# Moving two heads' score products side by side in TensorE's order, in a two-block transformer kernel

## The reference

```python
mod_x = jnp.split((jax.nn.silu(c) @ ada_w[layer] + ada_b[layer])[:, None, :], 6, axis=-1)
...
s = jnp.einsum('bqhd,bnhd->bhqn', q, k).astype(jnp.float32) * (HEAD_DIM ** -0.5)
p = jax.nn.softmax(s, axis=-1)
...
return jnp.einsum('bhqn,bnhd->bqhd', p.astype(v.dtype), v)
```

## Time and profile before

| | |
|---|---|
| median of three runs | 3044.91 us (3044.56 to 3044.98) |
| profiled execution, its time | 3045.68 us |
| its span | 3043.9 us |
| TensorE matmul busy | 2769.8 us (91%) |
| GpSimd busy | 1871.4 us (61%) |
| ScalarE busy, VectorE busy | 1490.2 us (49%), 1044.2 us (34%) |
| mean granted clock | 0.952 |
| at0, first scores to last transposed output | 219.6 to about 400.9 us |
| at1, the same | 932.6 to about 1056.7 us |

### The profile page before, as it was taken

How to read it: one execution, slowest core, us unless ns; L and a number is a source line. 1 busy time by engine, 2 the same in 40 slices (tenths; PEclk the granted TensorE clock), 3 DMA queues, 4 the chain that set the end, 5 groups by cost and what they waited for, 6 DMA issues and landing times.

```text
span 3043.9 us, 54209 instructions
## 1 busy us (share of the span) xinstructions
PE 2769.8 (91%) x19868; PEld 2566.2 (84%) x19868; DVE 1044.2 (34%) x2456; ACT 1490.2 (49%) x2604; POOL 1871.4 (61%) x789
## 2 busy tenths in 40 slices
PE   4999999999988989998889987899888899889897
PEld 2887778999976789997889987899878899778897
DVE  3124534111144521224333364333342333442334
ACT  4326744434444544444455565455545455454555
POOL 5426646878854668872458855388634588524685
PEclk8999999999998999998999998999999999989998
DMA  6224434545533445541235533255423355313453
GB/s 237 90 70 146 139 111 139 180 162 183 184 112 111 166 137 182 186 153 63 98 126 183 181 118 109 92 170 182 138 77 111 106 184 179 125 56 111 135 182 125
DMA packets 115044, 421.48 MB, mean 138 GB/s; under 512 B 12768, under 2 KB 13792, under 8 KB 114400
## 3 DMA queue, kind: packets, MB, share of 16 engines
q1 hardware_dynamic: 114336, 413.39, 40.5%
q10 hardware_dynamic: 576, 6.23, 0.5%
HBM read 418.52 MB, written 1.05 MB: 138 GB/s over the span
## 4 chain that ended last, share of the span: by engine, by line
issue 43%; PE 28%; POOL 25%; DVE 3%; ACT 1%; POOLq 1%; ACTq 0%; DVEq 0%
POOL ring_low L1922 25%; PE bank L544 8%; PE bank L545 8%; PE bank L546 8%; PE bank L725 1%; PE bank L752 1%; PE bank L660 1%; PE bank L657 1%; POOLq L1925 0%; DVE rstd L1416 0%; PE bank L768 0%; ACT ring_high L1014 0%; PE bank L739 0%; ACT scr L1111 0%; POOLq L1921 0%
## 5 line engine op out<-in xcount | busy, mean ns | idle before, releaser
L1922 POOL TENSOR_TENSOR ring_low<-ring,ring_high 128x1024 fp32r<-128x1024 f32 x785 | 1871.2, 2405 | 1150.0 <-ACT ring_high L1014 790.0
L544 PE MATMUL bank<-high,ring_high 128*128 128x256 f32 (+1 forms) x4052 | 1210.1, 299 | 148.6 <-DVE low L1478 73.0
L545 PE MATMUL bank<-low,ring_high 128*128 128x256 f32 (+1 forms) x4052 | 1191.5, 294 | 0.0
L546 PE MATMUL bank<-high,ring_low 128*128 128x256 f32 (+1 forms) x4052 | 1190.5, 294 | 0.0
L544 PEld LDWEIGHTS bank<-high,ring_high 128*128 128x128 f32 x4052 | 800.5, 198 | 172.8 <-DVE low L1478 77.3
L545 PEld LDWEIGHTS bank<-low,ring_high 128*128 128x128 f32 x4052 | 800.6, 198 | 10.8 <-issue 1.2
L546 PEld LDWEIGHTS bank<-high,ring_low 128*128 128x128 f32 x4052 | 799.8, 197 | 8.7
L1212 ACT ACTIVATE ring_high<-ring 128x1024 fp32r<-128x1024 f32 x462 | 479.0, 1051 | 33.9 <-PE bank L544 33.9
L1014 ACT ACTIVATE ring_high<-ring 128x1024 fp32r<-128x1024 f32 x323 | 334.7, 1052 | 124.6 <-PE bank L544 93.5
L544 PE MATMUL bank<-hid_high,ring_high 128*128 128x256 f32 x1232 | 351.0, 285 | 9.7 <-DVE hid_low L1683 9.7
L545 PE MATMUL bank<-hid_low,ring_high 128*128 128x256 f32 x1232 | 350.3, 284 | 0.0
(11 more groups left out here) (177 smaller groups left out, 2970.1 us busy)
## 6 DMA issues: line engine op xcount, KB each, us to landing
ring<-in_units SPq DMA_DIRECT2D x785, 512.0 KB, 3.3
xt<-in_x ACTq DMA_DIRECT2D x1, 2048.0 KB, 13.9
nbias<-in_bias ACTq DMA_DIRECT2D x1, 1536.0 KB, 8.1
consts<-in_consts ACTq DMA_DIRECT2D x1, 1472.0 KB, 8.2
vt<-in_mem ACTq DMA_DIRECT2D x1, 1024.0 KB, 7.6
out_x<-xt SPq DMA_DIRECT2D x8, 128.0 KB, 1.7
cols<-in_cols SPq DMA_DIRECT2D x1, 711.0 KB, 8.0
```

What stands on the lines that cost most here:

```text
L544: first = pe.matmul(out, w[0], x[0], start=start, stop=False, **more)
L545: pe.matmul(out, w[0], x[1], start=False, stop=False, **more)
L546: return first, pe.matmul(out, w[1], x[0], start=False, stop=stop, **more)
L1922: pool.tensor_tensor(whole(ring_low, u), whole(ring, u), whole(ring_high, u).bitcast(fp32), ALU.subtract).then_inc(unit_ready, 1)
```

## The change

TensorE's order: `scores(s+1, 1)` moves up behind `scores(s+1, 0)`, ahead of the transposes of head 1, and the modulation products of slot 3s, which stood between the two heads' scores, move behind the transposes of head 1. ScalarE's order: the copy of head 1's transposed probabilities moves ahead of `exps(s+1, 0)`, and `exps(s+1, 1)` moves ahead of the work of slot 3s+1. VectorE's, GpSimd's and SyncE's orders stay as they are. Only at0 and at1 (`shallow`) change; for the other attentions the order comes out as before.

```diff
@@ TensorE, attention @@
                         transposes(s, 0)
                         if shallow:
                             scores(s + 1, 0)
-                            fill(3 * s)
+                            scores(s + 1, 1)
                         transposes(s, 1)
-                        if shallow:
-                            scores(s + 1, 1)
-                        else:
+                        if not shallow:
                             scores(s + 2, 0)
                             scores(s + 2, 1)
+                        fill(3 * s)
                         if s:
                             out_t(s - 1)
@@ ScalarE, attention @@
                         out_pt(s, 0)
+                        out_pt(s, 1)
                         if shallow:
                             exps(s + 1, 0)
-                            ada_rest(3 * s)
-                        out_pt(s, 1)
+                        ada_rest(3 * s)
                         if s:
                             out_high(s - 1)
...
-                        ada_rest(3 * s + 1)
                         if shallow:
                             exps(s + 1, 1)
                         else:
                             exps(s + 2, 0)
                             exps(s + 2, 1)
+                        ada_rest(3 * s + 1)
                         ada_rest(3 * s + 2)
```

## The result

The changed kernel takes 3083.43 us (median of four runs, 3079.72 to 3095.89) against 3044.73: 38.7 us slower. The ratio of all runs together is 1.0135, 95% interval 1.0105 to 1.0165 (the two medians alone give 1.0127). The prediction was 3059, with 3035 to 3081. The profiled execution took 3079.72, 34.0 more than that of before. Its trace is read here, and it is the fastest of the four.

A forecast was written before the change was run, and what follows sets the result against it. TensorE's own work and the chain to unit u+3 were taken to bound the steps equally. 3045.68 - 8.9 us of savings + 23.7 us of clock falls = 3060.5, so 3059 for the median, range 3035 to 3081.

The forecast's parts named there:

- The overlap: In at0 and at1, both heads' scores run side by side at the price of one, saving 1.91 us per 512-key head.
- The chain to u+3: Head 0's scores, VectorE, exponentials, rounding, GpSimd, modulation unit u+3: not moved in at1, taken up at 9.75, gap about 2.5 us.
- The signs: New profile: scores x8 at 1.98, 2 to 3 us GpSimd wait, clock under 0.94 in at1, 0.96 in at0, slow values.
- The savings without falls: Paired scores in at0 and at1 save time before any loss through the clock: -8.9 us in all.
- The falls: Idle gaps lower TensorE's clock: half of nine at 4.9 us, half of two at 1.7, together +23.7 us.
- the heavy steps: Steps 1, 2, 8 to 10 of at0 and 1 to 6 of at1 (512-key scores, whole group): together -0.7 us.
- Rival A: None or one of the gaps lowers the clock, leaving only the savings: 3036 us; chance 0.17.
- Rival D: All heavy gaps are followed by a fall of the clock: +38.6 us, 3083; chance 0.08.
- From 1070 us on: The rest of the kernel, behind about 1070 us, stays as before, only shifted in time.

The follow-up runs named there:

- e1_filled: Changed kernel with extra TensorE products, later overwritten, filling the idle gaps ahead of late units; 3042.30 us against 3045.43, ratio 0.9989.
- e2_early: Changed kernel with ScalarE's rounding of slot 3s's first two units moved ahead of head 0's exponentials; 3022.46 us, ratio 0.9925.
- e9_ahead_sums: e5_ahead with VectorE's two additions of modulation columns moved to the next step, behind head 1's offsets; 3011.69 us, ratio 0.9888.
- e7_half: Changed kernel with half as many extra products ahead of each late unit as in e1_filled; 3049.46 us, ratio 1.0019.
- e10_two_gaps: e1_filled without the filling in steps 2 and 5 of at1; 3046.87 us, ratio 1.0002.
- e3_tensor_only: Changed kernel's TensorE order with ScalarE's order of before; 3055.33 us, ratio 1.0029.
- e5_ahead: Changed kernel with ScalarE rounding the next group's unit u+3 a group ahead in both attentions; 3055.96 us, ratio 1.0029.

## Why the prediction was right or wrong

**The overlap** was right: eight scores 1.99 us at the high clock, 3.79 at the low one; with 256 keys 1.14. The chip does not behave here as the packing part of "TensorE: Matmul & The Clock Gate" in the Trainium skill would have it. (A head is four products, of which strict order would let only the last run beside the first of the next head; a pair would then cost about 3.3 us, not 2.9. The measured 1.99 excludes both.)

**The chain to u+3** was right in at1 and in steps 1, 2 and 9 of at0. Exponentials at 4.67, GpSimd at 7.33, u+3 taken up at 9.73 instead of the 9.75 named; the gaps are 2.56 to 2.70 where "about 2.5" was said, and 2.17 in at0's steps 1 and 2 ("about 2.1"). In steps 8 and 10 of at0 it was wrong: the gaps are 3.06 and 3.37 where "about 2.4" was said, because the chain itself got longer by 1.2 and, in e1_filled at the high clock, 1.1 us. e2_early and e9_ahead_sums turn at1's gap into the saving, which shows that this chain made it.

**The signs** came as named: granted clock 0.89 in at0 and 0.76 in at1 (under 0.96 and 0.94), the L623 wait in the middle of its block, values at 6.4 to 6.9 us in some steps and 3.68 in others.

**The savings without falls** were too high. At0's steps 4 to 7 gave 4.7 us (4.1 forecast), steps 12 to 14 gave 1.0 (2.1), and step 7 of at1, to which the prediction gave no term, takes 2.5 us more even with the gaps filled (13.45 against 10.99 us, to the end of the last turned output): it has no scores to compute, and where its first unit used to fill the time until head 1 could be transposed, TensorE now waits and starts on that unit 3.3 us into the step instead of 0.9. Steps 8 and 10 of at0 are 2.1 us longer together, where the prediction had a small saving. The sum without falls was to be -8.9 us; e1_filled measured -3.1 in all and -2.7 in the two attentions.

**The falls** are the step that failed: one in two of eleven gaps, at 4.9 us or 1.7, was to cost 23.7 us in all; the trace has ten falls worth 39.8 us (26.4 in at1, 13.4 in at0). That falls would come, and by which mechanism, was right; the term was too small. The number: of the eleven gaps of the heavy steps seven fell, not five or six, which is well within such a guess, but three more fell where no gap had been counted, in both step 0s and in step 3 of at0 (1.76 us). For the step 0s only the time was costed, not what TensorE would wait for, and step 3 has no term in the sum at all, though it holds a whole group. The price: 5.3 us for a fall in at1 (26.4 / 5), above the 4.9 taken and inside 4.4 to 6.2, and 4.8 and 6.4 measured alone; in at0 4.6 in steps 9 and 10, and 1.6 in step 2, where 1.7 was taken.

So the prices were nearly right, and the number was too small: of the missing 16.1 us about 7 are six falls at 4.9 instead of half of nine, about 8 the three falls where no gap was counted (some 5.3, 1.8 and 1.3), and the rest is the price. Together at1 got 27.7 us longer instead of the 12.8 that its terms add up to, at0 9.4 instead of 2.0. For the profiled execution the miss adds up: 3079.72 against the 3060.5 of the sum is 19.2 us, of which the falls are 16.1 (39.8 less 23.7), the smaller savings 6.2, and the rest of the kernel -3.1. The median of the runs lies another 3.7 above the profiled one, where the prediction had put it 0.8 below and rounded down.

**Rival A** (no falls, 3036) is out for this kernel. By the table on why this matters on the same page of the Trainium skill, gaps of up to about 3 us would be harmless; here a gap of 1.76 had a fall behind it, and one of 3.06 had none. **Rival D** (all fall, 3083) has the right time by luck: not all of eleven gaps fell but ten of fourteen, and the savings were smaller. The range's upper end, 3081, left out just that case.

**From 1070 us on** nothing was to change, and the part behind at1 is 3.9 us shorter. 3.5 us of it arise between 1377 and 1441 us of the old trace, where a0t's low stretch is half as long here. No run says why; it is 10.2 to 20.5 us long in the traces.

What stays open is what decides whether a gap is followed by a fall. e7_half and e10_two_gaps show that length matters (none of seven at 1.5 to 1.8 us in at1, two of two at 2.69 in the profiled execution), the pair 1.76 and 3.06 that it isn't all; in e9_ahead_sums even a gap of 0.99 at the end of at0 has a low stretch of 3.4 us behind it. The number of falls seems to change from run to run: the changed kernel's times go with the mean granted clock (3079.72 at 0.941, 3095.89 at 0.935), so do those of e3_tensor_only (3042.24 at 0.952, 3067.55 at 0.943), and e10_two_gaps has its two groups. But only one execution of each kernel was profiled, so all counts of falls here are counts of one execution.

## What to carry to other kernels

Before work on the limiting engine is made denser, find what it will wait for next: if the chain behind that isn't made shorter in the same change, the saving turns into an idle gap, and here such gaps cost 39.8 us through TensorE's clock, where the denser order could give 21 in the eleven heavy steps (11 x 1.91). Where a gap can't be avoided, look at what stands behind it: in this kernel a fall cost 1.6 us where the 512-column products stood behind the gap and 5 to 6 where the 64-column values did. And when GpSimd becomes busy at a new moment, look for VectorE's small operations between tiles outside PSUM at that moment.

## What the runs showed of the hardware

VectorE's additions whose inputs both lie outside PSUM stood still while GpSimd worked. In e5_ahead 128x8 takes 2.3 us and ends within 0.05 us of an operation of GpSimd, in e9_ahead_sums the same takes 0.17. In e9_ahead_sums L1569 (128x4, 0.16 in the median) takes 1.82 us and ends at 998.93, GpSimd's operation at 998.91; L1608, with an input in PSUM and 32 times as many elements as an addition of 128x8, takes 0.42 in the same operation. The Trainium skill, "SBUF — State Buffer", in the section on the two sides of SBUF, says that VectorE and GpSimd share a pair of ports as an exclusive lock, held for a whole instruction, and that a VectorE operation with two SBUF inputs needs it. By that rule the additions should be blocked in full and the one with an input in PSUM not, and the trace agrees.

The price of a fall of the clock went with what stood behind the gap: 1.6 us with eight 512-column products there, low for 3.4 us; 4.8 to 6.4 with 64-column values, low for 10 to 14 us.
